# Fewer operands in Pool's running sum of squares, more in TensorE's

## What is computed

```python
def rms_norm(x, g):
    xf = x.astype(jnp.float32)
    y = xf * lax.rsqrt(jnp.mean(xf * xf, axis=-1, keepdims=True) + EPS)
    return (y * g.astype(jnp.float32)).astype(x.dtype)

def swiglu_ffn(h, w_up, w_down):
    gate, up = jnp.split(h @ w_up, 2, axis=-1)
    return (jax.nn.silu(gate) * up) @ w_down

x = x + 0.5 * swiglu_ffn(rms_norm(x, g_ffn1[l]), w_up1[l], w_down1[l])
```

## Time and profile before

| | us |
|---|---|
| median of 3 runs | 5113.91 (5113.07 to 5114.38) |
| profiled execution | 5113.42 |
| its span, first to last instruction | 5111.6 |
| TensorE busy | 4584.9 (90%) |
| VectorE busy | 2911.2 (57%) |
| ScalarE busy | 1820.3 (36%) |
| Pool busy | 596.7 (12%) |
| Pool's 70 adds of L247 | 70.5 + 23.4 |
| mean granted TensorE clock | 0.942 of full speed |

### The profile page before, as it was taken

One profiled execution on the slowest core, in us unless ns is written; L12 is line 12 of the kernel. 1 busy time (PEld: TensorE's weight loads), 2 busy tenths in 40 slices (PEclk: granted clock), 3 DMA queues, 4 the chain that ended last, 5 costly groups with the idle time before them and its releaser, 6 DMA issues.

```text
span 5111.6 us, 64788 instructions
## 1 busy us (share of the span) xinstructions
PE 4584.9 (90%) x22059; PEld 3848.4 (75%) x22059; DVE 2911.2 (57%) x4600; ACT 1820.3 (36%) x2890; POOL 596.7 (12%) x631
## 2 busy tenths in 40 slices
PE   7999888899999999988899987897646799999999
PEld 6887776678878877767788775686535699999998
DVE  4426566444344364664443584453798666666666
ACT  3225333332232254333222322232218644444444
POOL 0000000000000000000000000010485322222221
PEclk9999999999999999999999976798879999999999
DMA  3222210122222222101222220030102577777776
GB/s 119 93 99 83 84 57 33 66 83 98 99 86 96 99 83 84 57 33 66 79 93 99 85 77 7 0 125 32 58 33 99 218 274 278 277 273 279 275 276 243
DMA packets 85575, 599.85 MB, mean 117 GB/s; under 512 B 10640, under 2 KB 11024, under 8 KB 18512
## 3 DMA queue, kind: packets, MB, share of 16 engines
q1 hardware_dynamic: 57456, 410.85, 22.2%
q0 software_dynamic: 27136, 162.28, 9.3%
q10 hardware_dynamic: 864, 25.17, 1.2%
HBM read 570.99 MB, written 27.26 MB: 117 GB/s over the span
## 4 chain that ended last, share of the span: by engine, by line
PE 65%; issue 14%; DVE 11%; ACT 5%; DVEq 3%; ACTq 1%; DMA 1%; POOLq 0%; POOL 0%; SPq 0%
PE PB L188 19%; PE PB L190 19%; PE PB L189 19%; DVE RS L1146 2%; PE PB L869 2%; PE PB L1057 1%; ACT STG L2303 1%; PE PB L858 1%; PE PB L1864 1%; DVE WL L169 1%; DVE PB L1748 1%; DVE NM L889 1%; DVEq L1750 1%; DVEq L2162 1%; DVE SC L2165 1%
## 5 line engine op out<-in xcount | busy, mean ns | idle before, releaser
L188 PE MATMUL PB<-XH,WH 128*128 128x512 f32 (+1 forms) x3552 | 1351.6, 381 | 115.4 <-DVE WL L169 80.6
L190 PE MATMUL PB<-XH,WL 128*128 128x512 f32 (+1 forms) x3552 | 1338.0, 377 | 0.0
L189 PE MATMUL PB<-XL,WH 128*128 128x512 f32 (+1 forms) x3552 | 1337.6, 377 | 0.0
L169 DVE TENSOR_TENSOR WL<-RAW,WH 128x1024 fp32r<-128x1024 f32 x520 | 643.9, 1279 | 520.2 <-ACT WH L161 505.0
L188 PEld LDWEIGHTS PB<-XH,WH 128*128 128x128 f32 x3552 | 675.0, 190 | 238.7 <-issue 89.2
L189 PEld LDWEIGHTS PB<-XL,WH 128*128 128x128 f32 x3552 | 674.6, 190 | 109.1 <-issue 4.8
L161 ACT ACTIVATE WH<-RAW 128x1024 fp32r<-128x1024 f32 x520 | 520.5, 1050 | 645.2 <-PE PB L190 614.1
L190 PEld LDWEIGHTS PB<-XH,WL 128*128 128x128 f32 x3552 | 673.1, 190 | 101.8
L247 POOL TENSOR_TENSOR SQ<-SQ 128x512 f32<-128x512 f32 x49 | 70.5, 1439 | 2446.5 <-ACT SQ L230 2435.4
L188 PE MATMUL PB<-WH,WGH 128*128 128x512 f32 x768 | 299.7, 390 | 11.9 <-DVE WGL L2442 11.9
L190 PE MATMUL PB<-WH,WGL 128*128 128x512 f32 x768 | 302.2, 393 | 0.0
(11 more groups left out here) (393 smaller groups left out, 7629.5 us busy)
## 6 DMA issues: line engine op xcount, KB each, us to landing
RAW<-weights SPq DMA_DIRECT2D x387, 1024.0 KB, 4.8
gate_matrix<-STG ACTq DMA_DIRECT2D x6, 4096.0 KB, 11.6
GM<-gate_matrix POOLq DMA_DIRECT2D x128, 192.0 KB, 5.5
X<-x SPq DMA_DIRECT2D x4, 512.0 KB, 6.5
UV<-rows,IDX POOLq DMA_INDIRECT x128, 5.8
out<-FIN SPq DMA_DIRECT2D x4, 512.0 KB, 2.6
MEMX<-mem POOLq DMA_DIRECT2D x1, 1024.0 KB, 5.1
SK<-sub_keys POOLq DMA_DIRECT2D x1, 1024.0 KB, 5.0
```

Source lines behind the costliest of these rows:

```text
L169: c.nc.vector.tensor_tensor(c.WL[p][:, cols], c.RAW[p][:, cols], c.WH[p][:, cols].bitcast(F32), ALU.subtract).then_inc(c.sem("w_split"), 1)
L188: c.nc.tensor.matmul(out, wh, xh, start=start, stop=False)
L189: c.nc.tensor.matmul(out, wh, xl, start=False, stop=False)
L190: return c.nc.tensor.matmul(out, wl, xh, start=False, stop=stop)
```

## The change

Pool now adds only the first five chunks (chunks 1 to 4 into chunk 0, four adds instead of seven). TensorE sums four operands instead of one: the added one (chunk 0) and the squares of chunks 5, 6 and 7, accumulating in the same PSUM bank; likewise each token block's product is done four times. TensorE therefore also waits for the eighth square (`sq_ready`), beside Pool's sum.

```diff
+POOLED = 5
+PARTS = (0, *range(POOLED, DC))
+
+
 def pool_sum(c, pool, v, N, width=S):
 
-    for k in range(1, DC):
+    for k in range(1, POOLED):
         pool.wait_ge(c.sem("sq_ready"), v * DC + (k + 1))
         carry_wait(c, pool)
         last = c.nc.gpsimd.tensor_tensor(N.SQ[:, 0, :width], N.SQ[:, 0, :width], N.SQ[:, k, :width], ALU.add)
-        if k < DC - 1:
+        if k < POOLED - 1:
             pool.drain()
     last.then_inc(c.sem("sq_sum"), 1)
 
 
 def pe_sum(c, pe, v, N, width=S, tokens=False):
 
+    pe.wait_ge(c.sem("sq_ready"), v * DC + DC)
     pe.wait_ge(c.sem("sq_sum"), v + 1)
+    carry_wait(c, pe)
     if tokens:
         for tb in range(width // P):
-            c.nc.tensor.matmul(c.PB[:, 5, tb:tb + 1], N.SQ[:, 0, tb * P:tb * P + P], c.ONES[:, 0:1],
-                               start=True, stop=True)
-    c.nc.tensor.matmul(c.PB[:, 4, :width], c.ONES[:, :], N.SQ[:, 0, :width], start=True, stop=True)\
-        .then_inc(c.sem("norm_sum"), 1)
+            for k in PARTS:
+                c.nc.tensor.matmul(c.PB[:, 5, tb:tb + 1], N.SQ[:, k, tb * P:tb * P + P], c.ONES[:, 0:1],
+                                   start=k == 0, stop=k == DC - 1)
+    for k in PARTS:
+        last = c.nc.tensor.matmul(c.PB[:, 4, :width], c.ONES[:, :], N.SQ[:, k, :width],
+                                  start=k == 0, stop=k == DC - 1)
+    last.then_inc(c.sem("norm_sum"), 1)
```

## The result

The changed kernel takes 5145.33 us (median of 4 executions, 5140.14 to 5148.08) against 5113.51 (4 executions, 5113.07 to 5114.38): ratio 1.0061, 95% interval 1.0043 to 1.0078. It is slower, by 31.8 us. The forecast was 5134.0 with a range up to 5143: the direction is right, the size is not, and the time lies 2.3 us outside the range.

The account below looks back on a forecast made before the run. TensorE was taken to bound the kernel, Pool's sum mattering only where TensorE waits for it. The ten norms' terms sum to +18.9, with one clock fall (1.7) +20.6, on the profiled 5113.42: 5134.0 us, range 5122 to 5143.

Parts of the forecast that it names:

- What bounds the kernel: Whole kernel: TensorE's time is on the path; Pool's sum matters only where TensorE waits for it, 28.7 us in all.
- the waits: TensorE's waits for Pool: none over 2 us at norms 1, 3, 6, about 2 at norm 7, 7.3 at norm 10.
- The clock staying up: Norm 1, an FFN norm: wait shrinks to 1.5 us, clock stays at 2.4 GHz, giving -4.6 us; otherwise -2.3.
- An operand at 0.86: TensorE's sum: each further fp32 operand of 512 columns costs 0.86 us, three more 2.6 us.
- (b): Rival, sums at all norms: further operands cost far less because the ones are the same weights; about 5120 or 5113; chance 0.05.
- A token product at 0.101: TensorE's token products: 0.101 us each at full clock, so 24 more cost 2.4 us a norm.
- Norms 2 and 5: Token norms of a mixer, no wait for Pool: +5.0 us each, plus one fall of the clock, 1.7, for both.
- Norm 7: Token norm of a mixer: TensorE starts 5.0 us earlier, but the clock falls during token products; +1.5 us.
- Norm 10: Last of the memory and choosing norms: wait 4.5 us shorter, still 7 us, clock down; +3.1 us.
- (a): Rival, norms 2, 5, 7, 10: short products keep the clock up as well as long ones; +11.7, 5125.1 us; chance 0.16.
- (c): Rival, norms 2, 3, 5, 6: fewer Pool adds speed VectorE's two-input instructions through shared ports; -8, 5126 us; chance 0.05.
- (d): Rival: clock falls twice in each of norms 2 and 5 and stays down through norm 7; +30.5, 5144 us; chance 0.17.

Follow-up runs that it names:

- second trace: The changed kernel run again, unedited, for more executions and another profile: 5145.00 us, ratio 1.0056; its profiled execution took 5147.6 us.
- the kernel in which the clock was made to hold in the bursts: Changed kernel with four token products before each operand, and 9 and 28 ordinary matmuls before TensorE's waits at norms 7 and 10: 5126.86 us, ratio 1.0026.
- filled waits: Changed kernel with ordinary matmuls, results overwritten, in front of TensorE's wait, 9 at norm 7 and 28 at norm 10: 5136.35 us, ratio 1.0043.
- Interleaving: Changed kernel with the same instructions reordered, four token products (one token block) ahead of each operand of the sum: 5142.61 us, ratio 1.0056.
- tokens from one operand: Changed kernel, but token products read only the added operand (chunk 0) while the sum keeps four operands: 5122.43 us, ratio 1.0018.

## Why the prediction missed, step by step

- **What bounds the kernel, the waits, the instruction counts: right.** The waits of norms 1, 3, 7, 10 came out as the steps said (norm 1: 1.81 us against 1.5; norm 10: 7.32 against 7.3; norm 7: 2.79 against about 2). VectorE's read of the first tile is at 36.77 instead of 37.3, 5.1 us earlier than before, and 4.3 of it are left at norm 2 (forecast 4.6). The clock staying up was the assumption, and no stretch at half clock stands there any more.
- **An operand at 0.86: right.** Three more cost 2.54 to 2.58 at norms 3 and 4 (2.6), so rival (b) is out: the same ones as weights make nothing cheaper.
- **A token product at 0.101: 0.109,** 3.49/32; 0.3 us a norm too little.
- **Norms 2 and 5: mis-sized.** Forecast 5.0 each and one fall, 1.7, for both: 11.7. The first trace has 13.9, the second 18.3. The step read "I take one fall" between bounds of 0 and two stretches each. In their place the first trace has a fall within norm 5's burst and a stretch behind norm 2, 1.7 us each; only the fall is to be laid to the block, for the stretch stands also in kernels without one. The second trace has a longer fall within norm 2's burst besides, 3.4 us, and 3.9 us more behind it, of which further stretches are at least a part.
- **Norm 7: the largest miss, +5.3 to 5.6 instead of +1.5.** I took the clock's fall at the moment at which it stood in the trace before, 2.35 us into the new burst. It came 0.9 us into it (0.2 us ahead of it in the second trace), so 24 products and the first three operands ran at 1.2 GHz: the burst is 1.9 us longer than my sum. That the clock is back about 5 us after the sums begin was right (5.1). Pool's fourth add ended 7.77 us after the first one's start instead of 7.07: 0.7. The rest, 1.1, lies behind the sum, where TensorE waits 2.06 us for VectorE's chunk instead of 0.70 and a new stretch at half clock begins at 2912.9. With the forecast's 1.5 these three give 5.2.
- **Norm 10: right in the first trace,** +3.7 with its own arrival against +3.1; the second has 2.3 more for norms 9 and 10 together.
- **The median against the profiled execution: not in the sum at all.** I put the change on one profiled execution, 0.5 from its median. The changed kernel's executions scatter over 8 us, and its first profile is the lowest of four. 5.2 of the 11.3 us between 5134.0 and 5145.3 are this.
- **Rivals.** (a), the clock holds, is refuted for the changed kernel, and the kernel in which the clock was made to hold in the bursts comes near (a)'s time: 5126.9 against 5125.1. (The 4.1 us in (a)'s term for norm 10 are in no row; with the 4.8 of norm 1 it would be about 0.3 dearer. In the changed kernel the clock was down until 10.8 us after that burst's start.) (c), relief of VectorE, shows nowhere: norm 3 adds 0.6 as priced, and VectorE's instruction of the earlier trace rows has the same median at norm 2, 1.16 us before and 1.15 after. (d), two falls at norms 2 and 5 and 1.2 GHz through norm 7, is nearest with 5144, and in the second trace nearly in its mechanism; it had 0.17, and the range stopped 1 us short of its own time. The chosen forecast and (d) differ only in how often the clock falls, and the trace before had nothing that told it: its longest block of products has eight.
- **Where rule and row were weighed.** The prediction set against the Trainium skill, TensorE: Matmul & The Clock Gate, section Why this matters for your kernels, which asks that no long idle gap lie between bursts. The traces show that keeping to it was not enough here: norm 7, with its gap down to 2.79 us, cost +5.3 and not -1.9, and at norm 5 of the second trace the clock fell with TensorE busy in all of the 6.6 us before. The row was the better guide; the forecast leant on it, and not far enough.

## What to carry to other kernels

A sum moved to TensorE costs there 0.86 us for each further 512 columns of fp32, so it is worth it only where TensorE waits longer for the slower engine than the added operands take: at one of ten norms here, with a smaller share at two more. Many one-column products in one block cost more than their count: put them behind wide matmuls, or between them if the clock is up when they start (with the clock down, putting them between cost 1.6 us more here), and look at the granted clock in the burst before you price one. Where a rare event such as a fall of the clock is in the sum, price it by the number of places at which it can happen, and take more than one execution for the difference of two traces. Before you lay a stretch at half clock to the change, look whether a trace without the change has it too.

## What the runs showed of the chip that I had not expected

- With no idle time from the first one-column fp32 product on, TensorE fell to 1.2 GHz 2.3 to 4.8 us after the block of 32 began, in the seven cases at norms 2 and 5 counted above and at norms 7 and 10 with filled waits (there 1.35 and 0.95 us idle before the block). Three blocks of 32 at norm 2 had no such fall.
- Interleaving has two faces: it spares the fall at 2.4 GHz, and at 1.2 GHz it delays the return, from 11.1 us after the burst's start to 17.4. Four operands without a break brought it back in 3.8.
- Pool's add of the same shape took 1.26 to 2.19 us at norm 7, and the pause ahead of its second add was 1.1 us in the changed kernel and 2.88 in the one with tokens from one operand. The fourth add so ended 7.1 to 10.1 us after the first one's start. The timeline of Pool in that last kernel, norm 7:

```profile
2866.35 1.31 POOL L251 TENSOR_TENSOR SQ<-SQ 128x512 f32<-128x512 f32 x1
2870.55 1.46 POOL L251 TENSOR_TENSOR SQ<-SQ 128x512 f32<-128x512 f32 x1 [2.88 <-issue]
2872.25 1.43 POOL L251 TENSOR_TENSOR SQ<-SQ 128x512 f32<-128x512 f32 x1 [0.24 <-issue]
2874.29 2.19 POOL L251 TENSOR_TENSOR SQ<-SQ 128x512 f32<-128x512 f32 x1 [0.61 <-issue]
```

What it waits for in "issue" there, and why only at norms 7 and 10, was not tried and stays open. So does why one execution of the changed kernel has the long fall at norm 2 and another has not.
